# Normalised rows kept without the norm's scale and shift, which are applied by channel where rows leave PSUM; the first pair's rows by one-hot products; gate rows summed by GpSimd

## The reference

```
ada = silu(c) @ w_ada + b_ada        # shift1, scale1, gate1, shift2, scale2, gate2: 6 x 1024
h   = x * (1 + scale1) + shift1
q, k, v, cb, cc, cx = split(h @ w_in)                 # 8 heads of 64, and a gated convolution
mix = concat(stick_breaking_attention(q, k, v), cb * conv3(cc * cx)) @ w_out
x   = layer_norm(alpha * x + gate1 * mix) * ln1_g + ln1_b
h2  = x * (1 + scale2) + shift2
group = top-1 of 4 (h2 @ w_router_group); experts = top-2 of the 8 in the group (h2 @ w_router_expert)
moe = sum over the 2 chosen experts of weight * (silu(h2 @ w_gate[e]) * (h2 @ w_up[e])) @ w_down[e]
out = layer_norm(alpha * x + gate2 * moe) * ln2_g + ln2_b
```

## Time and profile before

| | before |
|---|---|
| median of 3 runs | 551.41 us (549.99 to 551.89) |
| span of the profiled execution | 550.1 us |
| TensorE matmul busy | 509.8 us (93%) |
| VectorE / ScalarE / GpSimd busy | 285.4 / 105.5 / 101.6 us |
| DMA, mean over the span | 308 GB/s, 169.22 MB |
| the chain that ended last | PE 61%, DVE 14%, DMA 11% |

### The profile page before, as it was taken

One profiled execution on the slowest core, in us unless ns is written; L12 is line 12 of the kernel. 1 busy time (PEld: TensorE's weight loads), 2 busy tenths in 40 slices (PEclk: granted clock), 3 DMA queues, 4 the chain that ended last, 5 costly groups with the idle time before them and its releaser, 6 DMA issues.

```text
span 550.1 us, 6473 instructions
## 1 busy us (share of the span) xinstructions
PE 509.8 (93%) x2516; PEld 274.5 (50%) x2516; DVE 285.4 (52%) x520; ACT 105.5 (19%) x173; POOL 101.6 (18%) x111
## 2 busy tenths in 40 slices
PE   3999999999999999999996999999998799898983
PEld 2445468744444444444583555555554355444531
DVE  4664999763937393263889732232222122213388
ACT  1000211233223231200232311111111111121030
POOL 2000000061306040030452111111211011210015
PEclk9999999999999999999997999999999899989998
DMA  8999679954640244269998999999999999999763
GB/s 254 358 361 352 207 237 309 309 212 153 227 155 1 77 146 174 75 245 418 413 391 310 388 405 420 414 416 417 414 417 416 416 415 416 416 416 418 312 251 153
DMA packets 71280, 169.22 MB, mean 308 GB/s; under 512 B 7902, under 2 KB 45842, under 8 KB 63056
## 3 DMA queue, kind: packets, MB, share of 16 engines
q1 hardware_dynamic: 64304, 152.22, 73.2%
q10 hardware_dynamic: 2480, 8.44, 4.0%
q0 software_dynamic: 4464, 8.12, 3.9%
HBM read 159.60 MB, written 17.30 MB: 322 GB/s over the span
## 4 chain that ended last, share of the span: by engine, by line
PE 61%; DVE 14%; DMA 11%; SPq 9%; issue 3%; ACT 1%; POOL 0%; DVEq 0%; POOLq 0%; ACTq 0%
PE ps L1622 17%; PE ps L1492 11%; PE ps L1538 10%; PE ps L1631 9%; DVE acc_rows L935 5%; SPq L414 4%; DMA w_gu<-in_w_up_dram 4%; PE ps L1612 3%; PE ps L1462 3%; DMA ada_stage<-in_w_ada_dram 3%; DMA w_stage<-in_w_in_dram 2%; PE ps L1481 2%; DMA y_tok<-y_dram 2%; PE ps L1526 2%; DMA y_dram<-ysb,slot_row 1%
## 5 line engine op out<-in xcount | busy, mean ns | idle before, releaser
L1622 PE MATMUL ps<-w_gu,xT 128*64 128x256 f32 x1024 | 119.3, 386 | 3.4 <-issue 1.6
L1622 PEld LDWEIGHTS ps<-w_gu,xT 128*64 128x64 f32 x1024 | 72.0, 138 | 40.5 <-issue 3.4
L1492 PE MATMUL ps<-hT,w_stage 128*128 128x512 f32 x192 | 84.8, 595 | 0.0
L1256 DVE TENSOR_TENSOR ysb<-ps,rows_gate 64x512 f32<-64x512 f32 x64 | 44.1, 689 | 61.8 <-PE ps L1631 61.3
L1631 PE MATMUL ps<-w_dn,hidT 128*64 128x512 f32 x256 | 62.9, 612 | 7.8 <-issue 6.1
L935 DVE SCALAR_TENSOR_TENSOR acc_rows<-ada_stage,csil,acc_rows 128x256 f32<-128x256 f32 x112 | 55.2, 493 | 4.0
L1247 DVE TENSOR_TENSOR hid<-ps,silu_sb 128x128 f32<-128x128 f32 x32 | 9.3, 292 | 91.9 <-ACT silu_sb L846 91.9
L1492 PEld LDWEIGHTS ps<-hT,w_stage 128*128 128x128 f32 x192 | 35.5, 190 | 41.0 <-issue 41.0
L1538 PE MATMUL ps<-wo,mixT 128*128 128x512 f32 (+1 forms) x144 | 55.6, 545 | 0.0
L1403 PE MATMUL ps<-hT,w_first 128*128 128x512 f32 x96 | 45.5, 621 | 0.9 <-DVE hT L961 0.9
L627 POOL DMA_INDIRECT y_dram<-ysb,slot_row x15 | 15.1, 1009 | 151.8 <-DVE ysb L1256 151.8
(11 more groups left out here) (213 smaller groups left out, 499.2 us busy)
## 6 DMA issues: line engine op xcount, KB each, us to landing
w_gu<-in_w_gate_dram SPq DMA_DIRECT2D x32, 1024.0 KB, 20.3
w_gu<-in_w_up_dram SPq DMA_DIRECT2D x32, 1024.0 KB, 23.3
w_dn<-in_w_down_dram SPq DMA_DIRECT2D x32, 1024.0 KB, 24.3
ada_stage<-in_w_ada_dram SPq DMA_DIRECT2D x16, 1024.0 KB, 7.8
w_stage<-in_w_in_dram SPq DMA_DIRECT2D x9, 1024.0 KB, 10.1
ada_in<-in_w_ada_dram SPq DMA_DIRECT2D x12, 512.0 KB, 9.5
y_dram<-zeros ACTq DMA_DIRECT2D x4, 1024.0 KB, 5.8
wo<-in_w_out_dram SPq DMA_DIRECT2D x2, 2048.0 KB, 13.3
```

The lines of the kernel that those rows point to most:

```text
L1256: ins = w.tensor_tensor(to[e * HD:(e + 1) * HD, b * 512:(b + 1) * 512], ps[b * HD:(b + 1) * HD, down_bank(y), :], gate2r[b * HD:(b + 1) * ...
L1492: ins = t.matmul(ps[:, 6], st[:, k, (f % 2) * P:(f % 2 + 1) * P], hT[:, k], start=k == 0, stop=k == KC - 1)
L1622: ins = t.matmul(ps[a * SLOTS:(a + 1) * SLOTS, GATE_BANK[e], 0:2 * P], rows_in[:, k, e * SLOTS:(e + 1) * SLOTS], weights[:, :, k, a * P:(a ...
```

## The change

1. xs keeps (x-mean)/deviation, made in one VectorE pass of 1024 for each tile. This row is what is stored for the gathers. The scale `a2c` and shift `b2c` are now vectors over channels, and channels lie on partitions once rows are transposed; so they are applied when rows leave PSUM, in eight ScalarE instructions of 128x128 for the router, and for a pair of experts in four on ScalarE and four on VectorE (`turn_out`), where one ScalarE copy of 128x1024 stood.
2. shift2 and scale2 are summed by TensorE into columns (`sum_mod2`, 16 products with one column of ones, in pair 0 of the heads). gate1 and gate2 are summed by GpSimd (`sum_row`, four all-reduces of 128x512): two after the masks of head 1, one after head 5, one after head 7. All of `spread_row`, `row_out` and the row arithmetic are gone.
3. Pair 0's rows are not gathered: one-hot matrices `hot_x` multiply the rows in SBUF (`first_rows`, 32 products of 128x128). The table of slots moves behind them, into the middle of gates(0) (`slot_table`).
4. x1 of tiles 0 and 1 is made by VectorE alone (`x1_stored`). Tiles 2 and 3 as before, but behind the first pair's rows.
5. SP may fill w_gu 0 and 1, w_dn 0 and 1 after the last `conv_proj` and the last `ada`; w_dn 5 is loaded early, w_gu 7 late.

Cut to its core:

```diff
...
-            sp.wait_ge(row_done, 6)
+            sp.wait_ge(conv_done, len(CONV_OUT))
             sp.wait_ge(ada_done, len(COLS) + NADACH - ADA1)
             load_gu(0)
             load_dn(0)
             load_gu(1)
-            sp.wait_ge(gate2_moved, 1)
             load_dn(1)
+            sp.wait_ge(row_summed, 4)
             sp.wait_ge(av_done, NH // 2)
             sp.wait_ge(conv_ev, len(CONV_OUT))
             for n in (2, 3):
                 load_gu(n)
                 load_dn(n)
+            load_dn(5)
             sp.wait_ge(out_done, TC)
             load_gu(4)
             sp.wait_ge(out_done, TC + 2)
             load_gu_part(6, 0)
             sp.wait_ge(out_done, NOUT)
             load_dn(4)
+            load_gu_part(5, 0)
             load_gu_part(6, 1)
-            for i in (0, 1):
-                sp.wait_ge(st_x1[i], 16)
-            load_gu_part(GU_RING - 1, 0)
             sp.wait_ge(logit_done, TC)
-            load_gu(5)
-            sp.wait_ge(x1_last, 2 + 2 * len(X1_BY_DVE))
-            load_gu_part(GU_RING - 1, 1)
+            load_gu_part(5, 1)
+            sp.wait_ge(xe_done, 1)
+            sp.wait_ge(x1_last, 4)
             for n in range(2):
                 sp.wait_ge(st_h2[n], 32)
-            load_dn(5)
+            load_gu_part(GU_RING - 1, 0)
             load_gu(GU_RING)
+            sp.wait_ge(x1_last, X1_STEPS)
+            load_gu_part(GU_RING - 1, 1)
...
+            def sum_row(r):
+                row, half = divmod(r, 2)
+                pool.wait_ge(ada_done, len(COLS) + 12 * row + 2 * half + 2)
+                g.partition_all_reduce((gate1r, gate2r)[row][:, half * 512:(half + 1) * 512], acc_gates[r][:], P,
+                                       bass.bass_isa.ReduceOp.add).then_inc(row_summed, 1)
             for h in range(NH):
                 pool.wait_ge(stay_done, h + 1)
                 mask(stay[h % 2], 1.0, stay_masked)
                 pool.wait_ge(take_done, h + 1)
                 mask(prob[h % 2], 0.0, take_masked)
-            pool.wait_ge(rows_ready, 1)
+                if h == 1:
+                    sum_row(0)
+                    sum_row(1)
+                if h == 5:
+                    sum_row(2)
+            sum_row(3)
...
-            inv_std_shift(0)
-            inv_std_shift(1)
-            x1_rows(1)
-            inv_std_shift(2)
-            inv_std_shift(3)
-            pool.wait_ge(mixg_done, NOUT)
-            g.memset(xg[0][:], 0.0).then_inc(xg_clear, 1)
+            for i in range(TC):
+                inv_std(i)
             for n in range(2):
                 pool.wait_ge(st_h2[n], 32)
-            pool.wait_ge(xg_clear, 1)
             pool.wait_ge(slots_ready, 1)
-            gather(0, xg[0], gathered[0])
-            pool.wait_ge(x1_done, 1)
-            pool.wait_ge(x1_last, 2 + len(X1_BY_DVE))
-            g.memset(xg[1][:], 0.0).then_inc(xg_clear, 1)
-            pool.wait_ge(xg_clear, 2)
+            pool.wait_ge(x1_last, X1_STEPS - 2)
             gather(1, xg[1], gathered[1])
-            pool.wait_ge(xe_done, 1)
-            gather(2, xg[rows_buffer(2)], gathered[rows_buffer(2)])
+            pool.wait_ge(x1_last, X1_STEPS)
+            gather(2, xg[2], gathered[2])
...
+            def affine(dst, src, k):
+                return s.activation(dst, src, ACT.Identity, scale=a2c[:, k:k + 1], bias=b2c[:, k:k + 1])
...
+            def turn_out(j):
                 act.wait_ge(xe_done, j + 1)
-                s.copy(xT[turned_buffer(j)].rearrange("p k t -> p (k t)"), flat[:, ROWS_AT:ROWS_AT + D]).then_inc(xe_ev, 1)
+                for k in range(KC // 2):
+                    ins = affine(xT[rows_buffer(j)][:, k], turned_rows(j, k), k)
+                ins.then_inc(xe_half_ev, 1)
...
+            for k in range(KC):
+                if k == 0:
+                    act.wait_ge(xe_half, 1)
+                if k == KC // 2:
+                    act.wait_ge(xe_done, 1)
+                affine(xT[0][:, k], turned_rows(0, k), k).then_inc(xe_half_ev if k < KC - 1 else xe_ev, 1)
...
+            def x1_stored(i):
+                dve.wait_ge(h2_done, i + 1)
+                dve.wait_ge(scaled, 2)
+                w.tensor_tensor(x1_rows[i][:], xs[:, i], g1r[:], ALU.mult).then_inc(x1_last, 1)
+                dve.wait_ge(x1_last, 2 * i + 1)
+                w.tensor_tensor(x1_rows[i][:], x1_rows[i][:], b1r[:], ALU.add).then_inc(x1_last, 1)
             for i in range(TC):
...
                 mix(TC + i)
                 if i == TC - 1:
                     mix(TC + i + 1)
                 moments(i)
...
+                if 0 < i < TC - 1:
+                    x1_stored(i - 1)
                 dve.wait_ge(rstd_done, i + 1)
...
+                w.tensor_scalar(xs[:, i], xs[:, i], mv[:, i, 0:1], rstd[:, i:i + 1], ALU.subtract, ALU.mult
+                                ).then_inc(h2_done, 1)
...
+            def first_hot(first, n, counted):
+                tiles = slice(first, first + n)
+                link(w.scalar_tensor_tensor(out=place[:, tiles], in0=mb[:, tiles, 0::HALF], scalar=-float(FILL), in1=counted,
+                                            op0=ALU.mult, op1=ALU.add))
+                w.tensor_tensor(hot_x[:, tiles], iota_m[:].unsqueeze(1).unsqueeze(1).to_broadcast([P, n, 2, SLOTS]),
+                                place[:, tiles].unsqueeze(3).to_broadcast([P, n, 2, SLOTS]), ALU.is_equal
+                                ).then_inc(hotx_done, 1)
+            def first_three():
+                dve.wait_ge(pos_done, 1)
+                first_hot(0, TC - 1, first_pair(ps[:, 6, 0:(TC - 1) * NE]))
...
+            column_values(0, lowv)
+            dve.wait_ge(pos_done, 2)
+            first_hot(TC - 1, 1, first_pair(ps[:, 5, (TC - 1) * NE:TC * NE]))
+            column_values(1, highv)
...
-            dve.wait_ge(normed, TC)
-            dve.wait_ge(scaled, 2)
-            for i in X1_BY_DVE:
+            dve.wait_ge(xe_done, 1)
+            for n in range(2):
+                dve.wait_ge(st_h2[n], 32)
+            for i in X1_HELD:
                 w.tensor_tensor(xs[:, i], xs[:, i], g1r[:], ALU.mult).then_inc(x1_last, 1)
             settle()
-            for n, i in enumerate(X1_BY_DVE):
-                dve.wait_ge(x1_last, 2 + n + 1)
+            for n, i in enumerate(X1_HELD):
+                dve.wait_ge(x1_last, X1_STEPS - 4 + n + 1)
                 w.tensor_tensor(x1_held(i), xs[:, i], b1r[:], ALU.add).then_inc(x1_last, 1)
...
+            def turn_out(j):
+                dve.wait_ge(xe_done, j + 1)
+                for k in range(KC // 2, KC):
+                    ins = w.tensor_scalar(xT[rows_buffer(j)][:, k], turned_rows(j, k), a2c[:, k:k + 1], b2c[:, k:k + 1],
+                                          ALU.mult, ALU.add)
+                ins.then_inc(xe_ev, 1)
...
+            def sum_mod2():
+                pe.wait_ge(ada_done, len(COLS) + 3 * D // CW)
+                for n in range(2):
+                    for k in range(KC):
+                        ins = t.matmul(ps[:, 7, n * KC + k:n * KC + k + 1],
+                                       acc_mod2[:, n].rearrange("q (p k) -> q k p", k=KC)[:, k], ones[:, 0:1],
+                                       start=True, stop=True)
+                ins.then_inc(mod_done, 1)
...
-            def spread_row(r):
-                src = acc_rows[:, r * 512:(r + 1) * 512] if r < 6 else gate2r[:, (r - 6) * 512:(r - 5) * 512]
-                t.matmul(ps[:, ROW_BANK[r]], ones[:], src, start=True, stop=True).then_inc(row_done, 1)
-            for r in range(4):
-                spread_row(r)
...
             transpose_h2(1)
             project_out(7)
+            route(1)
+            transpose_h2(2)
             project_out(8)
-            transpose_h2(2)
-            route(1)
-            pe.wait_ge(gate2_moved, 1)
-            pe.wait_ge(mixg_done, 2 * TC - 1)
-            spread_row(6)
             route(2)
-            transpose_h2(3, halves=2)
-            route(3, halves=2)
-            pe.wait_ge(mb_done, 2)
-            pe.wait_ge(mixg_done, NOUT)
+            keep_busy(2)
+            transpose_h2(3)
+            route(3)
...
+            def first_rows(c, k):
+                t.matmul(turned_rows(0, k), by_channel(xs[:, c])[:, k], hot_x[:, c].rearrange("p e s -> p (e s)"),
+                         start=c == 0 and k % 4 == 0, stop=c == TC - 1, skip_group_check=True)
             m2d = mb.rearrange("p c e -> p (c e)")
...
+            pe.wait_ge(mb_done, 1)
+            count_before(6, TC - 1, True).then_inc(pos_done, 1)
+            pe.wait_ge(hotx_done, 1)
+            for c in range(TC - 1):
+                if c == 1:
+                    pe.wait_ge(mb_done, 2)
+                    count_before(5, TC, False)
+                    for n in range(TC):
+                        ins = t.matmul(ps[:, 5, P:P + NE], ones_b[:], mb[:, n], start=False, stop=n == TC - 1, skip_group_check=True)
+                    ins.then_inc(pos_done, 1)
```

(22 more changed lines are left out.)

338 lines of the change are left out of this document (154 added, 184 removed).

## The result

The changed kernel takes 572.75 us (572.38 to 573.01), the kernel before 551.65 us beside it: ratio 1.0388, 95% interval 1.0367 to 1.0409. It is 21 us slower; I had predicted 4.6, and the range ended at 562. One more execution of the changed kernel took 2973.77 us, as one of the kernel before did later on with 1848.61; neither is in a range or a ratio here, and what held them up isn't known. The profiled execution has a span of 570.2 us against 550.1, so +20.1.

The account below looks back on a forecast made before the run. The weight stream reaching expert 29 bounds the kernel. gates(1) ends 6.7 us later (5.5 wait, 1.2 clock), earlier loads return 2.1: 4.6 on a 550.1 us span, plus 1.3 to the median, gives 556.0 us, range 548.5 to 562.

Parts of the forecast that it names:

- What bounds it: Expert stage: the end is set by when the stream of expert weights reaches expert 29.
- sum_mod2: Attention, TensorE: 32 instructions take 3.7 us, less 0.5 idle, so everything after moves 3.2 us later.
- First pair's products: Behind the router: 48 one-hot instructions take 5.6 us, so gates(0) starts at 300.6 us, 3.0 earlier.
- rival 4: First pair: products run at half clock, 5.6 us more, gates(0) not earlier, 561.6 us; chance 0.08.
- The added wait: Slot table inside gates(0) delays hidden(0): gates(1) starts 5.5 us later after 8.5 us TensorE idle, plus 1.2 for clock.
- Last tile to marks: Router's end: one pass gains 0.4 us, one-hots and counts cost 0.9; marks complete at 294.5 us.
- Early loads: SP starts weight loads 13 us earlier; the fuller ring buys the missing 0.8 MB, 2.1 us.
- GpSimd: Attention heads: sums over partitions at 3.7 us each fit the 19.8 us window, so nothing on the path.
- The rival's danger: Attention: GpSimd's sums at 9.9 us hold the heads, all later by 9.9 us, 565.9 us; chance 0.12.
- Pairs 1 to 15: Later expert pairs: eight evictions instead of one ScalarE copy lie beside other work and cost nothing.
- no change: First pair: the delay is small, gates(0) at 298 us and no clock loss, 552.2 us; chance 0.22.
- Rival 1: Weight stream: the faster case; 2.7 MB of later weights that slipped ahead come back, 7 us, 549.0 us; chance 0.15.

Follow-up runs that it names:

- e5: Changed kernel, with only the last VectorE instruction of a chunk writing strided, so sum_mod2 reads a contiguous operand: 568.16 us, 1.0317.
- e13: Changed kernel, with shift and scale summed by GpSimd behind head 3 and brought over by DMA, replacing the sixteen products: 566.09 us, 1.0253.
- e1: Changed kernel, with all 64 VectorE accumulations writing channels of one k side by side, so sum_mod2 reads a contiguous operand: 573.41 us, 1.0384.
- e9: e7 with VectorE's overflow one-hots moved behind the second expert's hidden row: 559.63 us, 1.0152.
- e7: Changed kernel with the edits of e5, e6 and e3 together: 557.17 us, 1.0127.
- e17: e7 with the first part of VectorE's overflow counts moved into its idle time ahead of the rows' eviction: 557.22 us, 1.0108.
- e2: Changed kernel, with the first pair's one-hot products reading contiguous channels (output not the reference's): 566.8 us, 1.0257.
- e6: Changed kernel, with the one-hot block as stationary operand, then evictions and eight transposes, slot table ahead of these: 563.89 us, 1.0246.
- e3: Changed kernel, with VectorE making the first expert's hidden row ahead of the overflow counts: 569.46 us, 1.0312.
- e15: Changed kernel, with VectorE's overflow counts moved ahead of its wait for the slot table: 567.34 us, 1.0284.
- e8: Changed kernel, with the first expert loads held until the first piece of the output projection, at 234.29 us: 572.26 us, 1.0400.
- e11: Changed kernel, with shift and scale summed by GpSimd behind heads 1 and 3 and brought over by DMA, replacing the sixteen products: 574.78 us, 1.0424.
- e4: Changed kernel, with the first pair's one-hot products reading at strides 4, 2, 3 and 1 for tiles 0 to 3 (output not the reference's): 567.71 us.

## Why the prediction was wrong

- **What bounds it: right.** The stream of weights sets the end; gates(29) start as expert 29's up weights land (496.78 + 22.84 us, 519.67), 20.3 us later than before.
- **sum_mod2: the step that failed first.** I priced 32 instructions at 3.7 us less 0.5, by rows with a contiguous operand. They took 7.54; with the half clock that lasts behind them (1.06 + 1.83 us more for two groups) the delay is 9.6 us instead of 3.2. e5 and e13 show it, worth 4 and 7 us of time. I had put the clock there at nothing. In this stretch it falls only where these products stand: the projection behind them took 7.58 to 8.86 us in all eight traces with the stride, 8.44 to 8.69 in e1, e5 and e9 with contiguous ones, but 7.03 in e7 and e17, which have contiguous ones too, and 7.03 in the seven traces without them. What in them makes it fall isn't settled.
- **First pair's products: the term that was mis-sized most.** 5.6 us at 0.117 each, with tile 0's hidden; measured 16.0 us at 0.25, from 297.97 to 313.99 with the counts, of which only the first 1.3 us lie ahead of the last marks. e2 (7 us) and e6 (8 us) show it. My upper bound of half clock (rival 4) came near the right price by luck, since a contiguous load at half clock takes 331 ns and a strided one at full clock 335. I gave it 0.08, and I had no row of a strided float32 product at all. gates(0) came at 313.99 instead of 300.6: 8.6 us of that lie here, 4.8 ahead.
- **The added wait: right, to 0.1 us.** gates(1) start 13.1 us after gates(0) (13.2 predicted), TensorE idle 8.76 (8.5 predicted). e3 and e15 show what it is worth: 4 to 6 us of time for 5.0 us less idle. The clock took 2.2 us from gates(1), the upper bound; I had taken 1.2.
- **Last tile to marks: right.** Marks were complete at 299.27 us instead of 294.5; sum_mod2's excess is 6.4 us, and the front part ran 1.6 us early (scores at 104.22, before at 105.80; within the scatter of this start, so luck): 4.8.
- **Early loads: the size wrong, the sign not shown.** I gave them 2.1 us. Expert 9's refill is 21.0 us later and gates(29) 20.3, so at most 0.7 us; e8 took 4.5 us of the head start away, and its last weights land within 0.1 us of the changed kernel's.
- **GpSimd: right,** 3.24 us a sum for 3.7 taken, and 5.6 us of idle ahead of the first. The rival's danger was another than I named: not late masks, but VectorE slowed around the sums (e11). The Trainium skill ("GPSIMD Engine Reference", section 3.2, Cross-partition) gives 247.7 us for a [128, 2048] reduction over partitions, by an estimate 62 us for 512. That figure is for `tensor_reduce` along the partition axis, another instruction than the all-reduce used here, which takes 3.24 us in this trace; I should not have carried it over. The Trainium skill (same page, section 2.1, Instruction dispatch) gives about 6 us at the first call of freshly loaded code; the 5.58 us ahead of the first sum fit that, and the third sum, at 182.06 us right behind a mask, has no such gap.
- **Pairs 1 to 15: right.** From gates(2) to gates(29) 183.2 us, 184.1 before, with eight scaled evictions a pair.
- **Rivals.** Neither the faster one nor no change came; the fourth came in effect, by the stride; the third didn't. Rival 1's surplus may be part of the 0.7 us and isn't told apart.

The sum, measured against the kernel before: gates(0) start 10.4 us later (8.0 of it is there when the attention part ends, 226.75 against 218.72), gates(1) 8.4 us more, their clock 2.2 more: 21.0 us at expert 9's refill, less 0.7 in the stream, 20.3 at gates(29). Against the predicted 6.7 us at the refill that is 14.3 us more: 8.6 from the first pair's products, 4.8 from ahead of them, 1.0 from the clock, less 0.1 in the wait.

## What to carry to other kernels

Price a product by a row with the same access pattern of its stationary operand, not only the same shape; a transpose is no stand-in for a float32 product. Where weights stream through a ring, follow the ring's refills: what counts is the start of the stage whose end frees a buffer, and which tensor's memory a buffer shares. Put GpSimd's sums over partitions where VectorE idles. Before moving a table behind a product, look at what stands in order behind the table on the engine that reads it.

## What the runs showed of the hardware

- Weight load of 128 x 128 float32 for products, at full clock: 190 to 192 ns contiguous, 196 at a stride of 2 elements, 261 at 3 (e4), 335 at 8; for a transpose with a stride of 8, 194. At half clock a contiguous load takes 331 ns (e2) and one at a stride of 8 still 335, so the stride costs little more there (3.79 against 4.19 us for 16 instructions).
- VectorE's accumulation of 128 x 256 float32, read and written at a stride of 128 elements: 673 against 485 ns (e1); with only the destination at that stride, 666 (e5).
- Beside GpSimd's sums over partitions some of VectorE's instructions are slow and others not: 2.65 us instead of 0.75 for one of the convolution's, 4.86 instead of 3.14 for a scan (e11), but another of the convolution's at its usual 0.75 us in the same stretch. Two sums took 7.75 us instead of 6.49 in e13.
- The granted clock fell to half behind 8.8 us of TensorE idle in the changed kernel (gates(1) 5.87 us for 3.67) and behind 3.0 + 0.9 us in e9 (gates(2) 5.82), but not behind 0.5 us in e17.
